# Head outputs of an attention loop: both PSUM halves copied by ScalarE and added by GpSimd

## The chip, the cores and the metric

One Trainium2 chip, one of its cores. The metric is the device time of one execution in microseconds; less is better. The kernel before took 729.84 us, the median of 3 runs (728.89 to 730.41).

## The reference

A decoder layer on a sequence of 1024 tokens and 1024 channels, in float32: an adaptive RMS norm, one projection that feeds a gated convolution and a sparse attention (an indexer picks at most 256 keys for a query), a group norm and gate on each, an output projection, a residual and a last norm. What the change touches is how the attention's values are summed and laid out; what is computed there is:

```
logits = jnp.einsum('bqhd,bqkhd->bqhk', q_b, k_sel).astype(jnp.float32) * att_scale
logits = jnp.where(valid[:, :, None, :], logits, -jnp.inf)
p = jax.nn.softmax(logits, axis=-1).astype(v.dtype)
return jnp.einsum('bqhk,bqkhd->bqhd', p, v_sel)
...
y_attn = group_rmsnorm(y_attn, gn_attn, N_HEADS) * jax.nn.silu(az)
y = jnp.concatenate([y_conv, y_attn], axis=-1) @ w_out
```

There are 8 heads of 64 dimensions. The kernel does not gather keys: it adds a bias of minus a large number to the logits of the keys that were not picked.

## The kernel before

The order of the work is written out by hand: each engine runs its own list of instructions in order, and semaphores alone join the lists. First come the norm and the projection (to about 500 us), then the attention loop (about 505 to 642 us), then the output projection.

Float32 products are made of float32r matmuls on a value's rounded part (names ending in H) and its remainder (ending in L). For the values, VV holds for a head 128 columns: the 64 of the rounded value and the 64 of the remainder. So the sum over keys comes out of TensorE as two groups of 64 PSUM rows, which must be added. In even heads rows 0 to 63 hold the one part and rows 64 to 127 the other, in odd heads the reverse, so that the sum of head h lands on the rows that its output has in ya (rows() in the code). ya[:, t, :] is the pair t of heads 2t and 2t + 1.

A head has 1024 queries in two halves (sb = 0, 1) of 512. A half is numbered g = 2h + sb, 0 to 15; its sum stands in PSUM bank 6 + sb. The loop goes over 96 chunks k, 12 to a head: 4 of the first half and 8 of the second, one for each block of 128 keys. For a chunk:
- TensorE transposes up to four 128x128 blocks of prob into bank 4 + k % 2 (turn, L749);
- ScalarE copies them rounded to phH (split_prob, L1041) and VectorE takes the remainder phL (low_prob, L1382);
- two chunks later TensorE multiplies both with VV (values, L762 and L763).

Two steps x = 2k and x = 2k + 1 belong to a chunk, and tables say at which step of a head the rest is put in the lists. It is for the next head: the logits of its 8 query blocks (logits, L671 and L672), their row maxima on VectorE (row_max, L1374, into nmx) and their exponentials on ScalarE (weights, L982, into prob). An exponential of block i covers (i + 1) x 128 keys, and each is followed by a read of its accumulator. For a block's logits TensorE waits for the exponential two before, which read the same banks. The transposes of a half begin when the exponentials of its four blocks are there.

Four steps after a half's last chunk, ScalarE copies the 64 rows that don't lie where the output does to tmp (other_half, L1050), which has one buffer, and one step later VectorE adds the other 64 rows to it (head_out, L1390), writes ya and raises s_o. For odd g this falls into the third chunk of the next head, ahead of the exponential of its last block (the odd place below); for even g into the third chunk of the second half (the even place). s_o frees tmp for ScalarE, frees the bank for TensorE's sum of the next head, and lets GpSimd square a pair's halves (pair_square, L1601). On the squares TensorE builds the group sums (group_sums, L780), and VectorE's gate multiplies ya in place (pair_gate, L1412) at an even place of heads 2, 4 and 6, where pair_add (L1421) takes the sums out. At the even places of heads 1, 3, 5 and 7 VectorE also copies denominators (keep_den, L1404) instead. At the even places of heads 2 to 5 ScalarE rounds a block of w_out (out_high, L1075), and GpSimd takes its remainder (out_low, L1606).

Of the kernel before, what the change touches and what calls it, by code (L numbers as in the profile page):

```python
# [23 lines left out]
NH = 8  # L24
NIH = 8
NT = 4
# [3 lines left out]
HALF = 512  # L30
# [13 lines left out]
ALU = mybir.AluOpType  # L44
ACT = mybir.ActivationFunctionType
# [102 lines left out]
EXP_AT = (10, 14, 17, 17, 22, 24, 27, 30)  # L148
FIRST_LOGITS = {2: 0, 3: 1, 4: 2, 5: 3, 6: 4, 10: 5, 12: 6, 14: 7}
TMP_AT, OUT_AT = 4, 5  # L150
LAST = 2 * STEPS * (NH - 1)

DSQ_AT = {24 * (2 * t + 1) + (9 if t < NT - 1 else 7): t for t in range(NT)}
# [32 lines left out]
def build(nc, a):  # L186
    with ExitStack() as ctx:
# [96 lines left out]
        tmp = at("tmp", [P, HALF], F32, 76)  # L284
# [5 lines left out]
        ya = at("ya", [P, NT, S], F32, 16)  # L290
# [15 lines left out]
        ps = ctx.enter_context(nc.psum_tensor("ps", [P, 8, HALF], F32))  # L306
# [42 lines left out]
        s_tmp = sem("s_tmp"); s_o = sem("s_o")  # L349
        s_dsq = sem("s_dsq"); s_dt = sem("s_dt"); s_dc = sem("s_dc"); s_dout = sem("s_dout"); s_din = sem("s_din")  # L350
        s_ysq = sem("s_ysq"); s_yss = sem("s_yss"); s_yln = sem("s_yln"); s_yrs = sem("s_yrs")
# [21 lines left out]
        def rows(h):  # L373

            return slice(HD * (h % 2), HD * (h % 2) + HD)
# [15 lines left out]
        OUTS = {2 * last_chunk(g) + 2 + OUT_AT: g for g in range(2 * NH - 1)}  # L391
# [197 lines left out]
        def _(pe):  # L589
# [4 lines left out]
            for j in range(2 * KT):  # L594
                mm = pe.matmul(ps[:, 0, j:j + 1], acc[:, P * j:P * j + P], onesF[:], start=(j == 0), stop=True,
                               skip_group_check=True)
# [6 lines left out]
            for t in range(NB):  # L603
                pe.wait_ge(s_xn, t + 1)
                for kt in range(3):
                    mm = turn_x(kt, t)
                    if t == NB - 1:
                        mm.then_inc(s_xtp, 1)
            for kt in range(3, KT):
                wait_h(pe, kt - 3)  # L610
                for t in range(NB):
                    mm = turn_x(kt, t)
# [81 lines left out]
            for kind, n in SCHEDULE:  # L694
                if kind == "unit":
                    unit(n)
                elif kind == "iwt":

                    pe.wait_ge(s_evac, 1)
                    for b in range(NB):  # L700
                        mm = pe.transpose(ps[:, 4, NIH * b:NIH * b + NIH], Tik[32:40, P * b:P * b + P], identF[32:40, 32:40])
                    mm.then_inc(s_iwt, 1)
                elif kind == "gate":

                    pe.wait_ge(s_gacc, KT)
                    for half in range(2):
                        mm = pe.matmul(ps[0:1, 6 + half, :], onesF[:], gacc[:, HALF * half:HALF * half + HALF], start=True, stop=True)
# [44 lines left out]
            def values(k):  # L752

                h, sb, j, c = CH[k]
                g = 2 * h + sb
                pe.wait_ge(s_pl, k + 1)
                if k == 0:
                    pe.wait_ge(s_vv, NT)
                if j == 0 and g >= 2:
                    pe.wait_ge(s_o, g - 1)  # L760
                out = ps[:, 6 + sb, P * c:HALF]
                pe.matmul(out, VV[:, j, h, :], phH[:, k % NPH, P * c:HALF], start=(j == 0), stop=False, skip_group_check=True)  # L762
                pe.matmul(out, VV[:, j, h, :], phL[:, k % 2, P * c:HALF], start=False, stop=(j == 4 * sb + 3),  # L763
                          skip_group_check=True).then_inc(s_pv, 1)
# [90 lines left out]
        def _(act):  # L855
# [187 lines left out]
            def other_half(g):  # L1043

                h, sb = g // 2, g % 2
                r, d = rows(h), rows(h + 1)
                act.wait_ge(s_pv, last_chunk(g) + 1)
                if g >= 1:
                    act.wait_ge(s_o, g)
                A(tmp[r, :], ps[d, 6 + sb, :], ACT.Copy).then_inc(s_tmp, 1)  # L1050

            def pair_cols(t, half):

# [100 lines left out]
        def _(dve):  # L1154
# [289 lines left out]
            for k in range(len(CH)):  # L1444
                for x in (2 * k, 2 * k + 1):
                    if x % 2:
                        low_prob(k)
                    for u in MAXES.get(x, ()):
                        row_max(u)
                    if x in OUTS:  # L1450
                        head_out(OUTS[x])
                    if x in DSQ_AT:
                        square_den(DSQ_AT[x])
                    if x in KEEP_AT:
                        keep_den(KEEP_AT[x])
                    if x in GATE_AT:
                        pair_gate(GATE_AT[x])
                    if x == LAST + 17:
                        pair_gate(NT - 1, 0)
                    if x in ADD_AT:  # L1460
                        pair_add(*ADD_AT[x])
                    if x in OUT_LOW_AT:
                        low_out(OUT_LOW_AT[x])
                if k == LAST // 2 + 3:
                    low_y(0, 0)
                if k == LAST // 2 + 5:
                    low_y(1, 0)
                if k == LAST // 2 + 11:
                    low_y(2, 0)
# [57 lines left out]
        def _(pool):  # L1527
# [68 lines left out]
            def pair_square(t, half):  # L1596
                pool.wait_ge(s_o, 4 * t + half + 3)
                if t:
                    pool.wait_ge(s_yss, 2 * t + half - 1)
                z = ya[:, t, HALF * half:HALF * half + HALF]  # L1600
                g.tensor_tensor(ysq[half][:], z, z, ALU.mult).then_inc(s_ysq, 1)  # L1601

            def out_low(ct):

                pool.wait_ge(s_woH, ct + 1)
                g.tensor_tensor(hL[:, ct, :], wo[:, ct, :], wo_high(ct).bitcast(F32), ALU.subtract).then_inc(s_woL, 1)  # L1606

            pair_square(0, 0)
            pair_square(0, 1)
            out_low(0)  # L1610
            pair_square(1, 0)
            out_low(1)
            pair_square(1, 1)
            out_low(2)
            pair_square(2, 0)
            out_low(3)
            pair_square(2, 1)
            pair_square(NT - 1, 0)
            pair_square(NT - 1, 1)


INPUTS = ("x", "positions", "w_ada", "w_out", "norm_f", "b_gate", "w_ik", "w_units", "vecs", "ident_f",
# [47 lines left out]
```

## Time and profile before

| what | value |
|---|---|
| median of 3 runs | 729.84 us (728.89 to 730.41) |
| the profiled execution | 727.33 us |
| its span, first to last instruction | 725.5 us |
| granted TensorE clock, mean | 0.991 |
| TensorE busy | 665.0 us (92%) |
| VectorE busy | 490.6 us (68%) |
| ScalarE busy | 365.0 us (50%) |
| GpSimd busy | 228.5 us (31%) |

Shares are over the whole span, in which the stages have different limits. PE is TensorE's matmuls, PEld its weight loads, DVE VectorE, ACT ScalarE, POOL GpSimd. L1050 is line 1050 of the kernel before. A row of the timeline gives start, duration, the instruction, and in brackets the idle time of its engine ahead of it with what ended it. The rows of neighbouring instructions on one engine can overlap a little.

### The profile page before, as it was taken

What the parts mean: (1) busy time and instruction counts of PE and PEld (TensorE: products, weight loads), DVE (VectorE), ACT (ScalarE), POOL (GpSimd) and SP (SyncE); (2) the same over time, 40 slices, a digit from 0 to 9 for tenths busy, and PEclk for the clock granted to TensorE, in tenths of its full rate; (3) what the DMA queues carried; (4) which work ended last, traced back from release to release, by engine and by line L of the source; (5) the groups of instructions that cost most, each with busy time, mean ns of one, the idle gap of its engine ahead of it and who ended that gap; (6) DMA issues with size and microseconds to landing.
All of it is one profiled execution on the core that took longest, in us unless ns stands there. A gap on an engine that the chain in (4) does not pass through costs nothing.

```text
span 725.5 us, 8772 instructions
## 1 busy us (share of the span) xinstructions
PE 665.0 (92%) x3170; PEld 548.3 (76%) x3170; DVE 490.6 (68%) x739; ACT 365.0 (50%) x550; POOL 228.5 (31%) x111
## 2 busy tenths in 40 slices
PE   0379998999999999999999999998998999989996
PEld 0468987878888888888888886886776777778885
DVE  4686814677788999999059753013898989586734
ACT  1484435555664142453543345434878877875212
POOL 0003323532233243658756579530012210000000
PEclk9999999999999999999999999998999999999999
DMA  8902289353323101111110262074853440121431
GB/s 344 414 34 86 57 194 173 116 159 112 96 85 97 63 30 58 44 44 58 32 56 29 87 204 88 30 166 112 293 126 88 117 117 0 60 85 61 174 117 58
DMA packets 22661, 79.14 MB, mean 109 GB/s; under 512 B 3738, under 2 KB 4058, under 8 KB 21596
## 3 DMA queue, kind: packets, MB, share of 16 engines
q1 hardware_dynamic: 22620, 78.60, 35.8%
q8 instruction: 25, 0.41, 0.2%
q14 instruction: 16, 0.13, 0.1%
HBM read 61.77 MB, written 13.41 MB: 104 GB/s over the span
## 4 chain that ended last, share of the span: by engine, by line
PE 71%; DVE 10%; DMA 7%; ACT 5%; issue 4%; SPq 2%; ACTq 0%; DVEq 0%
PE ps L632 15%; PE ps L634 15%; PE ps L633 15%; PE ps L811 4%; PE ps L812 4%; PE ps L813 4%; PE ps L749 4%; DMA iqs<-hlL 3%; PE ps L690 2%; PE ps L691 2%; PE ps L671 2%; PE ps L672 2%; DMA xin<-in_x 2%; DVE phL L1382 2%; DMA wa<-in_w_ada 2%
## 5 line engine op out<-in xcount | busy, mean ns | idle before, releaser
L632 PE MATMUL ps<-hH,wH 128*128 128x512 f32 (+1 forms) x592 | 229.4, 388 | 3.5 <-issue 2.3
L633 PE MATMUL ps<-hL,wH 128*128 128x512 f32 (+1 forms) x592 | 227.4, 384 | 0.0
L634 PE MATMUL ps<-hH,wL 128*128 128x512 f32 (+1 forms) x592 | 227.3, 384 | 0.0
L1532 POOL TENSOR_TENSOR wL<-raw,wH 128x1024 fp32r<-128x1024 f32 x37 | 94.3, 2550 | 185.1 <-ACT wH L866 185.1
L632 PEld LDWEIGHTS ps<-hH,wH 128*128 128x128 f32 x592 | 111.4, 188 | 25.6 <-issue 6.6
L634 PEld LDWEIGHTS ps<-hH,wL 128*128 128x128 f32 x592 | 111.4, 188 | 21.2
L633 PEld LDWEIGHTS ps<-hL,wH 128*128 128x128 f32 x592 | 111.5, 188 | 19.0
L1374 DVE CUSTOM_DVE_ANT_0 ps<-ps,bias 128x128 f32<-128x128 f32 (+3 forms) x64 | 48.7, 761 | 45.6 <-PE ps L672 43.7
L1382 DVE TENSOR_TENSOR phL<-ps,phH 128x512 fp32r<-128x512 f32 (+1 forms) x96 | 52.7, 554 | 21.9 <-ACT phH L1041 17.6
L1021 ACT ACTIVATE relu<-ps,wabs 128x384 f32<-128x384 f32 (+5 forms) x48 | 40.2, 848 | 42.5 <-PE ps L691 19.6
L1268 DVE SCALAR_TENSOR_TENSOR score<-relu,wsgn,score 128x384 f32<-128x384 f32 (+5 forms) x42 | 49.7, 1184 | 16.3 <-ACT relu L1021 13.6
L749 PE MATMUL ps<-identF,prob 128*128 128x128 f32 x288 | 50.7, 287 | 8.5 <-ACT prob L982 4.1
L1289 DVE TENSOR_SCALAR_CACHE_REDUCE above<-score,srch 128x384 bf16<-128x384 f32 (+5 forms) x60 | 56.8, 946 | 2.1
L1041 ACT ACTIVATE phH<-ps 128x512 fp32r<-128x512 f32 (+1 forms) x96 | 46.2, 489 | 20.7 <-PE ps L749 19.4
L982 ACT ACTIVATE prob<-ps,nmx 128x128 f32<-128x128 f32 (+3 forms) x64 | 47.3, 739 | 16.5 <-DVE nmx L1374 16.5
L749 PEld LDWEIGHTS ps<-identF,prob 128*128 128x128 f32 x288 | 35.3, 145 | 24.8 <-DVE phL L1382 13.2
L1601 POOL TENSOR_TENSOR ysq<-ya 128x512 f32<-128x512 f32 x8 | 8.8, 1103 | 138.8 <-DVE ya L1390 138.8
L812 PE MATMUL ps<-hL,yH 128*128 128x512 f32 x128 | 49.9, 390 | 0.0
L866 ACT ACTIVATE wH<-raw 128x1024 fp32r<-128x1024 f32 x37 | 39.0, 1054 | 21.2 <-DMA raw<-in_w_ik 12.1
L762 PE MATMUL ps<-phH,VV 128*128 128x512 f32 (+1 forms) x96 | 39.3, 409 | 0.0
L671 PE MATMUL ps<-ks,qs 128*128 128x512 f32 (+2 forms) x96 | 35.5, 370 | 3.0 <-ACT prob L982 1.8
L763 PE MATMUL ps<-phL,VV 128*128 128x512 f32 (+1 forms) x96 | 33.7, 352 | 0.0
(205 smaller groups left out, 1088.4 us busy)
## 6 DMA issues: line engine op xcount, KB each, us to landing
raw<-in_w_units SPq DMA_DIRECT2D x36, 512.0 KB, 3.4
wa<-in_w_ada SPq DMA_DIRECT2D x8, 1024.0 KB, 8.8
ks<-qk_halves SPq DMA_DIRECT2D x32, 256.0 KB, 5.6
xin<-in_x SPq DMA_DIRECT2D x8, 512.0 KB, 12.6
gw<-in_w_ada SPq DMA_DIRECT2D x8, 512.0 KB, 4.3
qs<-qk_halves SPq DMA_DIRECT2D x16, 256.0 KB, 4.1
wo<-in_w_out SPq DMA_DIRECT2D x8, 512.0 KB, 9.4
xe<-in_x SPq DMA_DIRECT2D x8, 512.0 KB, 4.0
```

Of the source, the lines that this page charges most:

```text
L632: pe.matmul(out, wH[:, n % 2, kt, :], hH[:, kt, cols], start=(kt == 0), stop=False)
L633: pe.matmul(out, wH[:, n % 2, kt, :], hL[:, kt, cols], start=False, stop=False)
L634: mm = pe.matmul(out, wL[:, n % 2, kt, :], hH[:, kt, cols], start=False, stop=(kt == KT - 1))
L671: pe.matmul(dst[:, o:e], q, ks1[h % 2][:, o:e], start=True, stop=False)
L749: mm = pe.transpose(ps[:, 4 + k % 2, P * b:P * b + P], prob_of(sb, b)[:, P * j:P * j + P], identF[:])
L812: pe.matmul(out, yH[b % 4][:, ct, :], hL[:, ct, cols], start=False, stop=False)
L982: A(prob_of(sb, i % 4), logit_bank(u), ACT.Exp, bias=nmx[:, u:u + 1], scale=-1.0, accum_out=den[:, h // 2, h % 2, i:i + 1]).then_inc(s_exp, 1)
L1268: v.scalar_tensor_tensor(score_of(i), relu[:, u % 2, 0:n], wsgn[:, i, h:h + 1], score_of(i), ALU.mult, ALU.add).then_inc(s_score, 1)
L1289: v.tensor_scalar(above[:, 0:(i + 1) * P], score_of(i), cand[:, b:b + 1], None, ALU.is_ge, ALU.add, accum_out=count[:, b:b + 1]).then_inc( ...
L1374: v.tensor_tensor_reduce(src, src, bias_of(i), -ATT_SCALE, 3.0e38, ALU.add, ALU.min, nmx[:, u:u + 1]).then_inc(s_mx, 1)
L1382: v.tensor_tensor(phL[:, k % 2, P * c:HALF], ps[:, 4 + k % 2, P * c:HALF], phH[:, k % NPH, P * c:HALF].bitcast(F32), ALU.subtract).then_in ...
L1532: g.tensor_tensor(wL[:, n % 2, :, :], raw[:, n % NRAW, :, :], wH[:, n % 2, :, :].bitcast(F32), ALU.subtract).then_inc(s_wL, 1)
```

## The change

For g = 0 to 13 (ADDED = 14), ScalarE copies both groups of 64 rows: one to tmp as before, and right behind it the other to its place in ya. It raises s_tmp after the second. GpSimd then adds tmp to ya in place and raises s_o. VectorE's sum is left out for these halves and stays for g = 14 and 15. TensorE waits for s_tmp, and no longer for s_o, before it reuses a half's bank. GpSimd's list is written in another order, since the adds now stand between the squares and the low parts of w_out.

```diff
+ADDED = 2 * NH - 2
...
                 if j == 0 and g >= 2:
-                    pe.wait_ge(s_o, g - 1)
+                    pe.wait_ge(s_tmp, g - 1)
...
-                A(tmp[r, :], ps[d, 6 + sb, :], ACT.Copy).then_inc(s_tmp, 1)
+                mm = A(tmp[r, :], ps[d, 6 + sb, :], ACT.Copy)
+                if g < ADDED:
+                    mm = A(ya[r, h // 2, HALF * sb:HALF * sb + HALF], ps[r, 6 + sb, :], ACT.Copy)
+                mm.then_inc(s_tmp, 1)
...
-                    if x in OUTS:
+                    if x in OUTS and OUTS[x] >= ADDED:
                         head_out(OUTS[x])
...
-            pair_square(0, 0)
-            pair_square(0, 1)
-            out_low(0)
-            pair_square(1, 0)
-            out_low(1)
-            pair_square(1, 1)
-            out_low(2)
-            pair_square(2, 0)
-            out_low(3)
-            pair_square(2, 1)
-            pair_square(NT - 1, 0)
-            pair_square(NT - 1, 1)
+            def head_add(n):
+
+                h, sb = n // 2, n % 2
+                r = rows(h)
+                pool.wait_ge(s_tmp, n + 1)
+                z = ya[r, h // 2, HALF * sb:HALF * sb + HALF]
+                g.tensor_tensor(z, z, tmp[r, :], ALU.add).then_inc(s_o, 1)
+
+            for t in range(NT):
+                if t:
+                    pool.wait_ge(s_ysq, 2 * t)
+                head_add(4 * t)
+                if 1 <= t <= 2:
+                    pool.wait_ge(s_o, 4 * t + 1)
+                    out_low(2 * t - 2)
+                    pool.wait_ge(s_woL, 2 * t - 1)
+                head_add(4 * t + 1)
+                if t < NT - 1:
+                    head_add(4 * t + 2)
+                pair_square(t, 0)
+                if 1 <= t <= 2:
+                    out_low(2 * t - 1)
+                    pool.wait_ge(s_woL, 2 * t)
+                if t < NT - 1:
+                    pool.wait_ge(s_ysq, 2 * t + 1)
+                    head_add(4 * t + 3)
+                pair_square(t, 1)
```

ScalarE's list before, from the odd place (g = 7) to the even place (g = 8); semaphores that an instruction waits for stand in brackets:

```order
L1050 ACTIVATE tmp<-ps 64x512 [waits s_o,s_pv]
L1041 ACTIVATE phH<-ps 128x256 [waits s_pv,s_tp]
L982 ACTIVATE prob_3_123,den<-ps,nmx 128x1024 [waits s_tp,s_mx]
L1041 ACTIVATE phH<-ps 128x128 [waits s_pv,s_tp]
L1041 ACTIVATE phH<-ps 128x512 [waits s_pv,s_tp]
L982 ACTIVATE prob_0_116,den<-ps,nmx 128x128 [waits s_tp,s_mx]
L1041 ACTIVATE phH<-ps 128x512 [waits s_pv,s_tp]
L1050 ACTIVATE tmp<-ps 64x512 [waits s_o,s_pv]
L1041 ACTIVATE phH<-ps 128x512 [waits s_pv,s_tp]
```

The same stretch of ScalarE's list now:

```order
L1051 ACTIVATE tmp<-ps 64x512 [waits s_o,s_pv]
L1053 ACTIVATE ya<-ps 64x512
L1042 ACTIVATE phH<-ps 128x256 [waits s_pv,s_tp]
L983 ACTIVATE prob_3_123,den<-ps,nmx 128x1024 [waits s_tp,s_mx]
L1042 ACTIVATE phH<-ps 128x128 [waits s_pv,s_tp]
L1042 ACTIVATE phH<-ps 128x512 [waits s_pv,s_tp]
L983 ACTIVATE prob_0_116,den<-ps,nmx 128x128 [waits s_tp,s_mx]
L1042 ACTIVATE phH<-ps 128x512 [waits s_pv,s_tp]
L1051 ACTIVATE tmp<-ps 64x512 [waits s_o,s_pv]
L1053 ACTIVATE ya<-ps 64x512
L1042 ACTIVATE phH<-ps 128x512 [waits s_pv,s_tp]
```

The copy to ya stands between tmp and the next phH at both places, with no wait of its own. The 1024-wide exponential is third behind tmp now, where it was second.

GpSimd's list before, from the first square on:

```order
L1601 TENSOR_TENSOR ysq_135<-ya 128x512 [waits s_o]
L1601 TENSOR_TENSOR ysq_136<-ya 128x512 [waits s_o]
L1606 TENSOR_TENSOR hL<-wo,hH 128x1024 [waits s_woH]
L1601 TENSOR_TENSOR ysq_135<-ya 128x512 [waits s_yss,s_o]
L1606 TENSOR_TENSOR hL<-wo,hH 128x1024 [waits s_woH]
```

GpSimd's list now, from the add of g = 3 on:

```order
L1618 TENSOR_TENSOR ya<-ya,tmp 64x512 [waits s_tmp,s_ysq]
L1605 TENSOR_TENSOR ysq_136<-ya 128x512 [waits s_o]
L1618 TENSOR_TENSOR ya<-ya,tmp 64x512 [waits s_tmp,s_ysq]
L1610 TENSOR_TENSOR hL<-wo,hH 128x1024 [waits s_woH,s_o]
L1618 TENSOR_TENSOR ya<-ya,tmp 64x512 [waits s_tmp,s_woL]
L1618 TENSOR_TENSOR ya<-ya,tmp 64x512 [waits s_tmp]
L1605 TENSOR_TENSOR ysq_135<-ya 128x512 [waits s_yss,s_o]
```

Each square now stands right behind the add that completes its half of the pair, and each low part of w_out stands in the longer gap between two adds.

## Rows read from the trace of the kernel before

**Rows 1.** One head: us, then busy us (instructions) of PE, PEld, DVE, ACT, POOL.

```profile
549.55:565.26 15.71, 14.07 (x87) 11.35 (x86) 13.75 (x32) 13.35 (x32) 3.38 (x2) 1.00 0.56 136
```

**Rows 2.** Waits from 510 to 645 us: total us, times, longest.

```profile
DVE phL L1382 <- ACT phH L1041: 13.1, 17, 2.4
...
PE ps L671 <- ACT prob L982: 1.8, 6, 0.3
```

**Rows 3.** Instructions on the tile tmp: min/median/max ns.

```profile
L1050 ACT ACTIVATE tmp<-ps x16: 588/592/596, 508.7 to 641.7; 64x512 f32<-64x512 f32 x16
L1390 DVE TENSOR_TENSOR ya<-ps,tmp x16: 672/684/695, 510.5 to 642.4; 64x512 f32<-64x512 f32 x16
```

**Rows 4.** Timeline, ScalarE, odd place: start us, duration us, instruction, idle before.

```profile
567.95 0.59 ACT L1050 ACTIVATE tmp<-ps 64x512 f32<-64x512 f32 x1
568.56 0.38 ACT L1041 ACTIVATE phH<-ps 128x256 fp32r<-128x256 f32 x1
568.84 1.11 ACT L982 ACTIVATE prob<-ps,nmx 128x1024 f32<-128x1024 f32 x1
569.84 0.20 ACT L982 ACTIVATION_READ_ACCUMULATOR prob<-ps,nmx 128x1 f32 x1
...
570.79 0.60 ACT L1041 ACTIVATE phH<-ps 128x512 fp32r<-128x512 f32 x1 [0.58 <-PE ps L749]
```

**Rows 5.** Timeline, VectorE, odd place.

```profile
568.50 0.14 DVE L1374 DVE_READ_ACCUMULATOR2_ANT nmx<- 128x1 f32 x1
...
571.42 0.69 DVE L1382 TENSOR_TENSOR phL<-ps,phH 128x512 fp32r<-128x512 f32 x1 [0.54 <-ACT phH L1041]
```

**Rows 6.** Timeline, TensorE, odd place.

```profile
570.09 0.66 PE L749 MATMUL ps<-identF,prob 128*128 128x128 f32 x4 [0.30 <-ACT prob L982]
```

**Rows 7.** Timeline, ScalarE, even place of head 3.

```profile
556.54 0.59 ACT L1050 ACTIVATE tmp<-ps 64x512 f32<-64x512 f32 x1
557.29 0.60 ACT L1041 ACTIVATE phH<-ps 128x512 fp32r<-128x512 f32 x1 [0.17 <-PE ps L749]
...
560.93 0.21 ACT L982 ACTIVATION_READ_ACCUMULATOR prob<-ps,nmx 128x1 f32 x1
```

**Rows 8.** Timeline, VectorE, even place of head 3.

```profile
558.64 0.69 DVE L1390 TENSOR_TENSOR ya<-ps,tmp 64x512 f32<-64x512 f32 x1
559.37 0.28 DVE L1404 TENSOR_SCALAR dT<-ps 16x128 f32<-16x128 f32 x1
```

**Rows 9.** Timeline, TensorE, even place of head 3.

```profile
561.21 0.48 PE L671 MATMUL ps<-ks,qs 128*128 128x512 f32 x1
```

**Rows 10.** Timeline, ScalarE, even place of head 1.

```profile
527.45 0.58 ACT L982 ACTIVATE prob<-ps,nmx 128x384 f32<-128x384 f32 x1 [0.29 <-DVE nmx L1374]
```

**Rows 11.** Timeline, ScalarE, even place of head 4.

```profile
573.39 0.60 ACT L1041 ACTIVATE phH<-ps 128x512 fp32r<-128x512 f32 x1 [0.54 <-PE ps L749]
...
577.34 0.20 ACT L982 ACTIVATION_READ_ACCUMULATOR prob<-ps,nmx 128x1 f32 x1
```

**Rows 12.** Timeline, VectorE, even place of head 4.

```profile
573.21 1.28 DVE L1412 SCALAR_TENSOR_TENSOR ya<-ya,vec,azs 128x1024 f32<-128x1024 f32 x1
...
575.00 0.67 DVE L1390 TENSOR_TENSOR ya<-ps,tmp 64x512 f32<-64x512 f32 x1
575.60 0.67 DVE L1421 TENSOR_TENSOR azs<-ps,dden 128x512 f32<-128x512 f32 x1
```

**Rows 13.** Timeline, TensorE, even place of head 4.

```profile
577.41 0.55 PE L749 MATMUL ps<-identF,prob 128*128 128x128 f32 x3
577.71 0.48 PE L671 MATMUL ps<-ks,qs 128*128 128x512 f32 x1
```

**Rows 14.** Timeline, GpSimd, squares and one low part.

```profile
570.32 1.04 POOL L1601 TENSOR_TENSOR ysq<-ya 128x512 f32<-128x512 f32 x1 [7.53 <-DVE ya L1390]
576.25 2.40 POOL L1606 TENSOR_TENSOR hL<-wo,hH 128x1024 fp32r<-128x1024 f32 x1 [4.88 <-ACT hH L1075]
...
643.14 1.54 POOL L1601 TENSOR_TENSOR ysq<-ya 128x512 f32<-128x512 f32 x1 [12.65 <-DVE ya L1390]
```

## The prediction

> **What bounds the kernel now.** I read first the waits and then the timeline, engine by engine, of the attention loop (about 505 to 642 us), since only that stage is touched. In one head's 15.71 us TensorE is busy 14.07, VectorE 13.75, ScalarE 13.35 and GpSimd 3.38 us [rows 1]. Three engines lie within 0.72 us of each other, so the busy shares name no bound, and the waits show a relay: VectorE waits 13.1 us in all for phH, and TensorE waits for exponentials [rows 2]. What counts is which engine hands over last at the points where the change edits a queue. There are two kinds, once a head each.
>
> *The odd place* (end of a head's second half: g = 1, 3, ..., 13). ScalarE runs tmp at 567.95, phH of 256 columns at 568.56, the 1024-wide exponential at 568.84, and its accumulator read ends at 569.84 + 0.20 = 570.04 [rows 4]. TensorE's four transposes start at 570.09, released by that exponential [rows 6]. The row maximum that the exponential also needs was there at 568.50 + 0.14 = 568.64 [rows 5], 0.20 us before it began: ScalarE's queue is late, not VectorE. Behind it VectorE idles 0.54 us until phH comes [rows 5], so time freed on VectorE here ends in that idle.
>
> *The even place* (g = 0, 2, ..., 12). ScalarE has idle time after tmp: 0.17 us in head 3 [rows 7], 0.54 us in head 4 [rows 11]. Here VectorE does the head's sum just ahead of work that TensorE wants, at 558.64 and 575.00 [rows 8, 12].
>
> **What is removed.** 14 of 16 sums on VectorE (684 ns median [rows 3]). From one start to the next such a sum holds VectorE 559.37 - 558.64 = 0.73 us in an odd head and 575.60 - 575.00 = 0.60 us in an even one [rows 8, 12]: about 9.3 us over the loop.
>
> **What is added on ScalarE.** 14 copies of 64x512 right behind tmp. The same shape from the same bank is tmp itself, 592 ns [rows 3], and the next instruction starts 568.56 - 567.95 = 0.61 us after it, while behind phH (0.38 us long) the next starts after 0.28 [rows 4]. So some instructions overlap the one ahead by 0.10 us and tmp does not. The new copy is not in the trace of before: its slot lies between 0.59 - 0.10 = 0.49 and 0.61 us. Unlike tmp it reads and writes the same 64 rows. In even heads these begin at partition 0, as phH's do, and I take 0.49; in odd heads they begin at 64, and I take 0.61, as for tmp. The Trainium skill, "ScalarE: Activation LUTs", in its passage on the ACTIVATE instruction's cost, has back-to-back ACTIVATEs overlap by about 93 ns. The trace agrees behind phH (0.10) and not behind tmp. By the page every copy would take 0.50 us, and the seven odd places would cost 3.5 us.
>
> At the odd place nothing covers the copy: phH, the exponential and TensorE's transposes all move by it. Heads 0, 2, 4, 6 give 4 x 0.49 and heads 1, 3, 5 give 3 x 0.61: **+3.8 us** (bounds 7 x 0.49 = 3.4 and 7 x 0.61 = 4.3). The VectorE slot freed there is worth nothing, for the reason above. If the exponential were late from VectorE instead, the cost would fall by no more than the 0.20 us in hand.
>
> At the even place the copy first fills ScalarE's idle time and VectorE's freed slot counts:
> - g = 2: the 384-wide exponential waits 0.29 us for VectorE [rows 10], so VectorE is late. I use head 3's rows for its first steps: phH comes 0.61 - 0.17 = 0.44 us later and 0.73 us of the sum goes: -0.3.
> - g = 6, 10: the same, but ScalarE then also rounds a block of w_out, and its exponential's read ends at 560.93 + 0.21 = 561.14 [rows 7], just ahead of TensorE's logits at 561.21 [rows 9]. These cannot come earlier than ScalarE: the gain is held there, 0.
> - g = 4, 8, 12: the 0.54 us idle takes the copy. VectorE is ahead by 0.60 us, the transposes (577.41) can move up, but the logits behind them (577.71) [rows 13] need the exponential whose read ends at 577.34 + 0.20 = 577.54 [rows 11]. Left is about 0.15 us each: -0.45.
> - g = 0: ScalarE has no second gap yet; 0.
>
> Bounds for the six: nothing, and the full slots 3 x 0.73 + 3 x 0.60 = 4.0 us.
>
> **GpSimd.** 14 adds of 64x512 with two inputs. The nearest rows are a 128x512 square, 1.04 us, and a two-input pass over 1024 columns, 2.40 us, half of which is 1.20 [rows 14]. I take 1.2. Queued behind the add are the squares; for them wait TensorE's sums and VectorE's gate, here at 573.21 [rows 12]. At the odd place both copies are done by 567.95 + 1.22 = 569.17, the add by 570.4, the square by 571.4, as before (570.32 + 1.04 = 571.36). All of it is covered, with 1.8 us in hand; at 2.4 us an add there would still be 0.6 left. ScalarE's next tmp waits for the add; it starts at 573.39 - 0.54 - 0.59 = 572.26 [rows 11, 3], 1.9 us after the add's end. The low parts of w_out now stand between adds, but only between a head's first and second half, where ScalarE's next tmp is some 12 us away. TensorE's wait for a free bank now ends at the copies instead of the sum; no wait on a sum shows among its waits, so 0.
>
> **Sum.** +3.8 - 0.3 - 0.45 = **+3.0 us**. The profiled execution took 727.33 us (725.5 of span and 1.8 around it); it comes to 730.4. The runs' median is 729.84, 2.5 above the profiled one, and I add the difference to the median: **732.8 us**. Own range of this case: 731.3 (low slot, deeper gains) to 734.6 (every copy 0.61, no gains).
>
> **Rivals.**
> - *The gains at the even places come in full* (no change). For it: TensorE's start may lag the matmuls' modelled rows, so that the limits of 0.1 us I read at 561.21 and 577.54 need not bind. Against: waits of logits on exponentials do show, 6 of them [rows 2]. 3.8 - 4.0 = -0.2: 729.6.
> - *VectorE is the bound and the odd places hide the copy* (faster). For it: after the odd exponential ScalarE idles 0.58 us [rows 4], as much as a copy, and a wait on several semaphores is put to the last by inference. Then only the 4.0 us of the even places count: 725.8. Against: the transposes start 0.05 us behind the read's end, too close for chance.
> - *GpSimd and VectorE block each other* (slower still). The last square beside a VectorE pass took 1.54 instead of 1.04 us [rows 14]. At g = 4, 8, 12 the new add becomes ready within 0.2 us of the gate on VectorE [rows 12]. If the add starts first and the gate must wait, that is 1.04 to 1.2 us three times, in a stretch where VectorE is late: +3.4, 736.2. It decides only where the add is first; by the rows (both copies done at 572.26 + 0.61 + 0.49 = 573.36, the gate at 573.21) the gate is. The Trainium skill, "SBUF — State Buffer", in its part on the engine side, calls the shared port pair an exclusive lock, whoever starts first holding it for the whole instruction, against VectorE passes with two SBUF inputs. By it an add that loses is late by the gate's 1.28 us, which the slack bears.
>
> **Chances.** Forecast 0.60, full gains 0.17, hidden copies 0.15, blocking 0.08. A change within 0.2% (1.5 us) is about what a measurement cannot tell from none. Faster is the third case and some of the second, 0.19; same the rest of the second and the low edge of the first, 0.16; slower 0.65. The range of 728.5 to 735.2 leaves out most of the hidden and the blocking case.
>
> **What the profile after would show.** VectorE's busy time 9.6 us less, ScalarE's 8.3 more, GpSimd's some 16 more. The copy's row at 0.59 us, the next instruction 0.49 or 0.61 behind it. At the odd places the 1024-wide exponential 0.5 to 0.6 us later against its row maximum, and TensorE's transposes with it. The step from odd place to odd place 0.3 to 0.6 us longer. The forecast is wrong if that exponential keeps its distance from the row maximum, if the head's period shrinks, or if the gates or sums wait for GpSimd's squares.

## The result, and the profile after

The changed kernel took 733.38 us, the median of 13 runs (730.23 to 739.08), against 728.02 us for the kernel before, measured beside it (726.11 to 731.16, 13 runs): ratio 1.0082, 95% interval 1.0067 to 1.0097. It is slower by 6.0 us by the ratio and by 5.4 by the medians. The forecast was slower by 3.0 us: the time lies in the forecast range, and the forecast size is half of the measured one. The forecast time of 732.8 us stood on the first three runs' median of 729.84; 3.0 on top of 728.02 would be 731.0.

The profiled execution took 733.8 us, with a span of 731.7 and a mean granted clock of 0.986. Line numbers are those of each kernel: L1051, L1053 and L983 after stand for L1050 (tmp), the new copy and L982 (exponential). First the instructions on ya and tmp (min/median/max ns):

```profile
L1053 ACT ACTIVATE ya<-ps x14: 590/592/595, 510.7 to 623.1; 64x512 f32<-64x512 f32 x14
L1618 POOL TENSOR_TENSOR ya<-ya,tmp x14: 1263/1275/2045, 511.3 to 623.7; 64x512 f32<-64x512 f32 x14
...
L1394 DVE TENSOR_TENSOR ya<-ps,tmp x2: 694/694/695, 634.8 to 648.6; 64x512 f32<-64x512 f32 x2
```

The copy takes 592 ns like tmp [rows 3], GpSimd's add 1275 ns, and two sums are left on VectorE. Next ScalarE's timeline at the odd place of g = 7, to be held against [rows 4]:

```profile
571.07 0.59 ACT L1051 ACTIVATE tmp<-ps 64x512 f32<-64x512 f32 x1
571.68 0.59 ACT L1053 ACTIVATE ya<-ps 64x512 f32<-64x512 f32 x1
572.29 0.38 ACT L1042 ACTIVATE phH<-ps 128x256 fp32r<-128x256 f32 x1
572.57 1.11 ACT L983 ACTIVATE prob<-ps,nmx 128x1024 f32<-128x1024 f32 x1
573.57 0.20 ACT L983 ACTIVATION_READ_ACCUMULATOR prob<-ps,nmx 128x1 f32 x1
...
574.52 0.60 ACT L1042 ACTIVATE phH<-ps 128x512 fp32r<-128x512 f32 x1 [0.58 <-PE ps L750]
```

The next instruction starts 0.61 us behind tmp and 0.61 behind the copy (head 3 is odd). The same stretch at g = 13, in head 6, which is even:

```profile
622.46 0.59 ACT L1051 ACTIVATE tmp<-ps 64x512 f32<-64x512 f32 x1
623.06 0.59 ACT L1053 ACTIVATE ya<-ps 64x512 f32<-64x512 f32 x1
623.55 0.37 ACT L1042 ACTIVATE phH<-ps 128x256 fp32r<-128x256 f32 x1
623.82 1.10 ACT L983 ACTIVATE prob<-ps,nmx 128x1024 f32<-128x1024 f32 x1
```

Here the copy holds ScalarE for 623.55 - 623.06 = 0.49 us. At g = 7 the idle time behind the exponential is 0.58 us as before: everything has moved by the copy, and no gap took it up. VectorE and TensorE at g = 7, against [rows 5, 6]:

```profile
571.65 0.14 DVE L1378 DVE_READ_ACCUMULATOR2_ANT nmx<- 128x1 f32 x1
...
575.15 1.53 DVE L1386 TENSOR_TENSOR phL<-ps,phH 128x512 fp32r<-128x512 f32 x2 [0.89 <-ACT phH L1042]
```

```profile
573.82 0.66 PE L750 MATMUL ps<-identF,prob 128*128 128x128 f32 x4 [0.89 <-ACT prob L983]
```

The row maximum was there at 571.79, 0.78 us before the exponential began; it was 0.20 before the change. TensorE stands idle 0.89 us ahead of its transposes, where it was 0.30; over the seven odd places it is 0.74 to 0.77 us in even heads and 0.89 to 0.91 in odd ones, where it was 0.29 to 0.31. VectorE's idle time has grown from 0.54 to 0.89 us: that is where its freed slot went, with the copy's delay.

The chain of waits says the same. Before, it came over VectorE's row maximum into the odd place (start, us, what):

```profile
568.50 0.14 DVE nmx L1374
568.64 0.42 DVE phL L1382
...
569.84 0.21 ACT prob L982
...
570.09 0.66 PE ps L749 x4
```

Now it stays on ScalarE's list:

```profile
570.83 0.13 ACT prob L983
...
571.07 0.59 ACT tmp L1051
...
571.68 0.49 ACT ya L1053
...
572.29 0.38 ACT phH L1042
572.67 0.31 ACT prob L983
...
573.57 0.21 ACT prob L983
...
573.82 0.66 PE ps L750 x4
```

The even place of head 3 (g = 6), ScalarE and then TensorE, against [rows 7, 9]:

```profile
559.50 0.59 ACT L1051 ACTIVATE tmp<-ps 64x512 f32<-64x512 f32 x1
560.10 0.59 ACT L1053 ACTIVATE ya<-ps 64x512 f32<-64x512 f32 x1
560.72 0.60 ACT L1042 ACTIVATE phH<-ps 128x512 fp32r<-128x512 f32 x1
...
564.02 0.23 ACT L983 ACTIVATION_READ_ACCUMULATOR prob<-ps,nmx 128x1 f32 x1
```

```profile
564.30 0.50 PE L672 MATMUL ps<-ks,qs 128*128 128x512 f32 x1 [0.29 <-ACT prob L983]
```

The idle 0.17 us behind tmp is filled, and the logits now wait visibly for the exponential, whose read ends at 564.02 + 0.23 = 564.25.

The even place of head 4 (g = 8), GpSimd and VectorE:

```profile
577.32 2.04 POOL L1618 TENSOR_TENSOR ya<-ya,tmp 64x512 f32<-64x512 f32 x1 [2.48 <-ACT ya L1053]
```

```profile
576.93 1.28 DVE L1416 SCALAR_TENSOR_TENSOR ya<-ya,vec,azs 128x1024 f32<-128x1024 f32 x1
```

GpSimd's add takes 2.04 us beside the gate instead of 1.28, and the gate keeps its 1.28 us [rows 12]. GpSimd bears the collision. The Trainium skill's rule of the shared port pair ("SBUF — State Buffer", engine side) agrees with this: the one that starts first keeps the pair for its whole instruction. The gate was first, with 0.89 us to go when the add began, and the add took 0.77 us longer.

**Where the time went.** The best ruler in these traces is the start of the 1024-wide exponential, once a head; between two of them lie one even and one odd place. Distances in us, worked out from the timelines:

| from, to | before | after | difference | places |
|---|---|---|---|---|
| span's start to head 0 | 499.46 | 501.07 | +1.61 | none |
| head 0 to 1 | 20.79 | 21.48 | +0.69 | g = 0, 1 |
| 1 to 2 | 15.71 | 16.16 | +0.45 | 2, 3 |
| 2 to 3 | 17.18 | 17.39 | +0.21 | 4, 5 |
| 3 to 4 | 15.70 | 16.47 | +0.77 | 6, 7 |
| 4 to 5 | 17.18 | 17.39 | +0.21 | 8, 9 |
| 5 to 6 | 15.70 | 16.45 | +0.75 | 10, 11 |
| 6 to 7 | 17.19 | 17.41 | +0.22 | 12, 13 |
| head 7 to the span's end | 106.59 | 107.88 | +1.29 | none |

From head 0 to head 7 the loop has lengthened by 3.3 us, where the forecast has 3.0. The other 2.9 us of the two traces lie where no edited instruction stands. Behind the last odd place (g = 13) TensorE's clock is lower. Its two waits there, of which the first was 0.89 us before too and the second 0.29:

```profile
623.62 0.33 PE L750 MATMUL ps<-identF,prob 128*128 128x128 f32 x1 [0.87 <-DVE phL L1386]
...
625.06 0.66 PE L750 MATMUL ps<-identF,prob 128*128 128x128 f32 x4 [0.77 <-ACT prob L983]
```

The windows (columns as in [rows 1], the granted clock ahead of the last two):

```profile
623.00:626.00 3.00, 1.61 (x10) 1.08 (x10) 1.63 (x7) 2.92 (x8) 1.27 (x1) 0.98 0.31 117
626.00:629.00 3.00, 2.61 (x7) 2.03 (x7) 1.08 (x2) 0.87 (x2) 0.00 (x0) 0.50 0.17 63
629.00:632.00 3.00, 3.00 (x19) 2.46 (x19) 1.47 (x3) 2.08 (x3) 0.00 (x0) 0.95 0.00 0
```

From 626 us on, for a little over 3 us, TensorE runs at half of full speed, the lower of its two levels, 1.2 against 2.4 GHz. The trace of before shows 1.00 there throughout. Both traces have the lower level at the loop's start as well, from about 500 and 503 us on, for some 7 us. The 1.61 us before the loop belong to instructions that the change leaves alone; there the window from 130 to 140 us shows 0.66 after, and the one from 120 to 130 us 0.83 before.

### The profile page after: what moved, and what is told of

It reads as the page before. It is cut to its first block, busy times and chain, and to the rows that moved or that the text cites. A ratio compares the mean times of both kernels' runs of the same rounds, so it can differ in the third digit from the quotient of the medians.

```text
span 731.7 us, 8796 instructions
## 1 busy us (share of the span) xinstructions
PE 668.1 (91%) x3170; PEld 550.7 (75%) x3170; DVE 486.0 (66%) x725; ACT 371.2 (51%) x564; POOL 248.9 (34%) x125
## 4 chain that ended last, share of the span: by engine, by line
PE 81%; ACT 8%; DVE 5%; issue 4%; DMA 2%; SPq 0%; ACTq 0%; DVEq 0%
PE ps L633 17%; PE ps L635 17%; PE ps L634 17%; PE ps L812 4%; PE ps L814 4%; PE ps L813 4%; PE ps L750 3%; DMA wa<-in_w_ada 2%; ACT prob L983 2%; PE ps L691 2%; PE ps L692 2%; PE ps L672 2%; PE ps L673 2%; PE ps L763 1%; PE ps L764 1%
## 5 line engine op out<-in xcount | busy, mean ns | idle before, releaser
L1618 POOL TENSOR_TENSOR ya<-ya,tmp 64x512 f32<-64x512 f32 x14 | 20.1, 1437 | 107.9 <-ACT ya L1053 107.9
L983 ACT ACTIVATE prob<-ps,nmx 128x128 f32<-128x128 f32 (+3 forms) x64 | 47.2, 739 | 13.4 <-DVE nmx L1378 12.9
L596 PE MATMUL ps<-onesF,acc 128*128 128x1 f32 x32 | 7.0, 352 | 29.5 <-DVE acc L1180 29.5
```

Of the source, the lines that this page charges most:

```text
L983: A(prob_of(sb, i % 4), logit_bank(u), ACT.Exp, bias=nmx[:, u:u + 1], scale=-1.0, accum_out=den[:, h // 2, h % 2, i:i + 1]).then_inc(s_exp, 1)
```

## The experiments

Three questions: whether ScalarE's place ahead of the exponential is the cost (theory S) or something of VectorE (V) or of load as such (L); whether the lower clock follows from the change (C); and whether a better placing beats both kernels. Each kernel was timed beside the kernel before, in 6 or 12 runs against 17 to 35 of it. Diffs are against the changed kernel; ADDED is the list of halves that ScalarE copies twice and GpSimd adds, and TensorE's bank wait and VectorE's list follow it. With an empty ADDED the kernel does the work of the one before, but GpSimd's list keeps its new order:

```diff
-                    pe.wait_ge(s_tmp, g - 1)
+                    pe.wait_ge(s_tmp if g - 2 in ADDED else s_o, g - 1)
...
-                    if x in OUTS and OUTS[x] >= ADDED:
+                    if x in OUTS and OUTS[x] not in ADDED:
...
             def head_add(n):
+                if n not in ADDED:
+                    return
```

**Even places alone.**

```diff
+ADDED = (0, 2, 4, 6, 8, 10, 12)
```

> ScalarE copies both halves and GpSimd adds only for even g (0 to 12); odd g as before. Theory S (the odd place costs one ScalarE slot, since the 1024-wide exponential stands behind the copy, and the even places give back little): with the odd places as before, the loop should take what the even places gave in the trace of the changed kernel, +0.2 (g = 0), -0.16 (g = 2), three times -0.28 (g = 4, 8, 12) and twice +0.15 (g = 6, 10): -0.5 us, ratio 0.998 to 1.001. Theory V (VectorE's freed time is what counts and the full slots of 0.60 to 0.73 us come in): -4 us, ratio 0.994.

Ratio 1.0005 (0.9991 to 1.0020). The distances from exponential to exponential changed by +0.26, -0.13, -0.07, +0.17, -0.08, +0.17, -0.07: +0.25 us in all, not -0.5. Theory V falls. S's figure was off too: the gains at g = 4, 8, 12 shrink from 0.28 to 0.07 or 0.08 us when VectorE still does the odd sums, so the places do depend on each other.

**Odd places alone.**

```diff
+ADDED = (1, 3, 5, 7, 9, 11, 13)
```

> ScalarE copies both halves and GpSimd adds only for odd g (1 to 13); even g as before. S: 0.49 us in heads 0, 2, 4, 6 and 0.61 in heads 1, 3, 5, +3.8 us in the loop, every distance from one 1024-wide exponential to the next longer by one slot. If in addition the granted clock falls behind the last odd place as in the changed kernel, 1.2 us more: ratio 1.005 to 1.007. V: the freed VectorE slots cancel it, ratio 1.000 or below.

Ratio 1.0068 (1.0047 to 1.0089), median 732.20 us. The distances grew by 0.57, 0.59, 0.46, 0.60, 0.45, 0.59, 0.44: +3.7 us, with the two sizes of the slot in turn. In the trace the clock behind the last odd place is at its lower level again, but over the 6 runs it is 0.991 in the mean, the same as in the 17 runs of the kernel before beside them. So the odd places hold nearly the whole cost, and here most of it without a lower mean clock.

**One copy more at the odd places, nothing taken off VectorE.**

```diff
+ADDED = ()
...
-                if g < ADDED:
+                if g in ADDED or g in (1, 3, 5, 7, 9, 11, 13):
```

> The kernel before with one more ScalarE copy behind tmp at every odd place: it writes the other half to ya, and VectorE then does its sum as before and writes over it. GpSimd adds nothing and VectorE is freed of nothing. S: the same as the odd half of the change alone, +3.8 us in the loop within 0.3, since the freed VectorE slot falls into its own idle time there. V: worse than that kernel by the seven VectorE slots, 4 to 5 us more, ratio 1.011 or above.

Ratio 1.0073 (1.0050 to 1.0097), median 731.59 us; +3.9 us in the loop, 0.2 from the run above. Whether VectorE is freed of seven sums there or not makes little difference while the even places are as before: the slot ends in its idle time. TensorE's row at one of these places reads as it does in the changed kernel:

```profile
571.52 0.66 PE L750 MATMUL ps<-identF,prob 128*128 128x128 f32 x4 [0.90 <-ACT prob L983]
```

**All but the last odd place.**

```diff
+ADDED = tuple(range(13))
```

> The changed kernel, but the half g = 13 (the last odd place) is summed by VectorE as before. S: 0.49 us less than the changed kernel in the loop, +2.8 against before. Theory C (the slower clock behind the last odd place, 1.24 us in the trace of the changed kernel, comes from TensorE's longer idle time there): no clock drop in that stretch, so 1.7 us less in all than the changed kernel, ratio 1.004 to 1.006. If the drop is chance, it shows here or in other kernels as often.

Ratio 1.0057 (1.0040 to 1.0074). No drop behind the last odd place, as expected, but one at another: the transposes that wait 0.90 us at g = 7 then run at the lower level.

```profile
572.95 1.05 PE L750 MATMUL ps<-identF,prob 128*128 128x128 f32 x4 [0.90 <-ACT prob L983]
...
574.23 1.06 PE L750 MATMUL ps<-identF,prob 128*128 128x128 f32 x4
```

```profile
571.00:573.00 2.00, 0.98 (x6) 0.41 (x4) 1.00 (x4) 1.98 (x5) 1.36 (x2) 1.00 0.91 252
573.00:576.00 3.00, 3.00 (x15) 3.00 (x16) 1.03 (x3) 1.66 (x6) 0.95 (x1) 0.51 1.04 235
576.00:578.00 2.00, 2.00 (x10) 1.26 (x10) 2.00 (x4) 1.43 (x3) 0.72 (x1) 0.88 0.77 170
```

Four transposes take 1.05 us instead of 0.66, and that distance is 19.01 us where the changed kernel has 17.39. So the drop is not bound to the last place; the expectation had named a drop elsewhere as the sign of chance. The last distance (g = 12 changed, g = 13 as before) is 16.95 us for 17.19: the gain of 0.24 is there although VectorE does the sum of g = 13. Set against the even places alone, it seems to hang on the sum of the odd place ahead, g = 11; no run tests that by itself.

**The copy behind the exponential.** At the odd places the copy to ya stands at step 7 instead of 4.

```diff
+COPY_AT = 7
...
                 mm = A(tmp[r, :], ps[d, 6 + sb, :], ACT.Copy)
+                if g in ADDED and g % 2:
+                    return
...
+                    if x in COPIES:
+                        late_copy(COPIES[x])
```

> The changed kernel, but at the odd places the copy to ya stands three steps later in ScalarE's list, behind the 1024-wide exponential and the phH of 128 columns; s_tmp is raised there. Theory S (the cost is the copy's place ahead of that exponential): ScalarE idles 0.58 us there, which takes 0.49 in even heads and all but 0.03 in odd ones, so the loop loses the 3.8 us again and keeps the even places' -0.4: 0.0 to -0.6 us against before, no longer TensorE wait, hence no clock drop at an odd place, ratio 0.998 to 1.001. Theory L (ScalarE's load as such counts, wherever the copy stands): +3 us or more, ratio 1.004 or above.

Ratio 0.9998 (0.9981 to 1.0015), median 727.80 us: the whole loss is gone with the same instructions, the same load on each engine and the same 14 adds on GpSimd. Its loop is 0.24 us shorter than before. Theory L falls and S stands. ScalarE at g = 7:

```profile
568.60 0.59 ACT L1053 ACTIVATE tmp<-ps 64x512 f32<-64x512 f32 x1
569.20 0.38 ACT L1044 ACTIVATE phH<-ps 128x256 fp32r<-128x256 f32 x1
569.48 1.11 ACT L985 ACTIVATE prob<-ps,nmx 128x1024 f32<-128x1024 f32 x1
570.48 0.20 ACT L985 ACTIVATION_READ_ACCUMULATOR prob<-ps,nmx 128x1 f32 x1
570.57 0.28 ACT L1044 ACTIVATE phH<-ps 128x128 fp32r<-128x128 f32 x1
570.87 0.59 ACT L1064 ACTIVATE ya<-ps 64x512 f32<-64x512 f32 x1
571.49 0.60 ACT L1044 ACTIVATE phH<-ps 128x512 fp32r<-128x512 f32 x1
```

The exponential is 0.28 us behind phH and 0.88 behind tmp (0.28 and 0.89 in [rows 4]), and the copy fills the 0.58 us that were idle. One place did lose: at g = 13 the late copy stands ahead of ScalarE's copies for the output projection, and TensorE waits 1.56 us where it waited 0.46. From the last exponential to the end this trace takes 107.82 us for 106.59, at full clock behind that wait.

```profile
623.00 0.47 PE L814 MATMUL ps<-hH,yH 128*128 128x512 f32 x1 [1.56 <-ACT yH L1101]
```

**TensorE kept busy while it waits.** The changed kernel with transposes that nothing reads. TensorE's wait for phL (s_pl) moves ahead of them, since they write the bank.

```diff
+                if k >= 2:
+                    pe.wait_ge(s_pl, k - 1)
+                if h and sb and j == 0:
+                    for b in range(6):
+                        pe.transpose(ps[:, 4 + k % 2, P * (b % 4):P * (b % 4) + P], identF[:], identF[:])
                 if j == 0:
                     pe.wait_ge(s_exp, NB * h + 4 * sb + 4 if k else NB)
-                if k >= 2:
-                    pe.wait_ge(s_pl, k - 1)
```

> The changed kernel with six more 128x128 transposes of the identity on TensorE at each odd place, put before its wait for the exponential; they are written to the bank that the next transposes overwrite, and nothing reads them. The wait for the exponential stays. S and theory C (the granted clock falls because TensorE stands idle longer at the odd places): the loop stays at +3.3 us, within 0.3, and no stretch at an odd place shows the lower clock, so the 1.2 to 1.6 us of that drop are gone: ratio 1.004 to 1.006. If the drop has nothing to do with that idle time, it stays, and the ratio is 1.007 to 1.009.

Ratio 1.0038 (1.0024 to 1.0052), median 730.33 us. In its trace every stretch from 510 to 726 us is at 1.00; the distances are those of the changed kernel within 0.04 us but the first (+0.18), and from head 7 to the end it is 106.59 us, as before the change. The mean clock of its 12 runs is 0.993; of the changed kernel's 13 it is 0.987, and of the 35 runs of the kernel before beside it 0.991. The filler is work added, and yet it wins back 0.44% of the 0.82%. It was expected to win less: 1.2 to 1.6 us, against 3.2 by the two ratios. As it also lifts the clock above that of the kernel before, it does more than take back what the longer waits cost.

**tmp behind the exponential as well, in the kernel before.**

```diff
+ADDED = ()
+TMP_ODD, OUT_ODD = 7, 8
```

> The kernel before with tmp three steps and the VectorE sum three steps later at the odd places, both behind the 1024-wide exponential. S: that exponential then waits for its row maximum, which comes only 0.20 us before ScalarE is free, so at most 0.2 us is won at each of seven places: -0.5 to -1.4 us, ratio 0.998 to 0.9995. If ScalarE's queue alone were the limit: a whole slot each, -4 us, ratio 0.994.

Ratio 1.0005 (0.9987 to 1.0022): nothing that can be measured, where 0.998 to 0.9995 was expected. The exponential now waits for its row maximum, as expected:

```profile
566.98 1.12 ACT L984 ACTIVATE prob<-ps,nmx 128x1024 f32<-128x1024 f32 x1 [0.48 <-DVE nmx L1379]
```

Six distances are shorter by 0.06 to 0.12 us each, 0.6 in all; the first one fell by 2.06 us (18.73), and this trace, alone of those so far, kept the full clock at the loop's start. 2.3 us came back behind head 7: tmp delays the output projection's copies (TensorE waits 1.08 us for them), and a stretch of a little over 3 us around 638 us is at the lower level.

**Late copies, and four even places.**

```diff
+ADDED = (1, 3, 5, 7, 9, 11, 13, 2, 4, 8, 12)
+COPY_AT = 7
```

> The late copy at the odd places, and at the even places the change only where the trace of the changed kernel showed a gain: g = 2, 4, 8, 12; g = 0, 6, 10 are summed by VectorE as before. S: 0.2 + 0.15 + 0.15 us less than the late copy at all 14, so -0.5 to -1.1 us against before, ratio 0.998 to 0.9995, the fastest of these. If the places depend on each other, no better than the late copy at all 14.

Ratio 0.9999 (0.9982 to 1.0016), no better than the late copy at all 14, though expected to be the fastest. Its loop is 1.0 us shorter than before, most in the distances with g = 4, 8 and 12 (16.92 for 17.18), but behind head 7 it takes 109.42 us against 106.59, with the lower clock from 621 to 628 us, where TensorE waits for the yH copies that stand behind the late copy:

```profile
622.00 0.76 PE L814 MATMUL ps<-hH,yH 128*128 128x512 f32 x1 [1.56 <-ACT yH L1101]
```

The late copy at all 14 has the same wait of 1.56 us and kept the full clock behind it, so such a wait does not always bring the drop.

**The same with the last odd place as before.**

```diff
-ADDED = (1, 3, 5, 7, 9, 11, 13, 2, 4, 8, 12)
+ADDED = (1, 3, 5, 7, 9, 11, 2, 4, 8, 12)
```

> Late copies at the odd places 1 to 11, g = 13 wholly as before (tmp ahead of the exponential, VectorE's sum), and ScalarE's two copies with GpSimd's add at the even places 2, 4, 8 and 12. The late copy at the last odd place held up ScalarE's yH copies and with them TensorE by about 1.1 us in the trace; that is mended. Theory S: -0.16 - 3 x 0.25 = -0.9 us in the loop and nothing lost behind it, ratio 0.997 to 1.000. If the even places' gains are within noise: 1.000.

Median 726.50 us against 727.42; ratio 0.9980 (0.9967 to 0.9994). It beats both kernels; against the one before the gain is small, 1.5 us by the ratio and 0.9 by the medians. In its trace the six distances from head 1 on are 0.8 us shorter, near the expected 0.9. But g = 2 gives nothing (15.72 for 15.71), and behind head 7 it takes 108.19 us for 106.59, where nothing was to be lost: TensorE is at the lower level from 637 to 641 us. This comes behind a wait that the kernel before has too, at full clock (the second row):

```profile
636.94 0.54 PE L814 MATMUL ps<-hH,yH 128*128 128x512 f32 x1 [1.94 <-DVE azs L1437]
```

```profile
637.84 0.47 PE L811 MATMUL ps<-hH,yH 128*128 128x512 f32 x1 [1.95 <-DVE azs L1421]
```

**Idle transposes in the kernel before, and in that last one.**

```diff
+                if k >= 2:
+                    pe.wait_ge(s_pl, k - 1)
+                if k == 0:
+                    pe.wait_ge(s_exp, NB - 1)
+                if k == 0 or h and sb and j == 0:
+                    for b in range(4 if k else 12):
+                        pe.transpose(ps[:, 4 + k % 2, P * (b % 4):P * (b % 4) + P], identF[:], identF[:])
...
-                if k >= 2:
-                    pe.wait_ge(s_pl, k - 1)
```

> The kernel before with idle transposes of the identity on TensorE: twelve at the start of the loop, after the seventh exponential of head 0, and four at each odd place ahead of the wait. Nothing else changes. Theory C: the lower clock that every trace but one shows at about 500 to 508 us (a loss of about 2 us, by the one trace without it: 18.73 against 20.79 us from the first to the second 1024-wide exponential) goes away or shrinks: ratio 0.996 to 0.999. If the filler only takes TensorE's time and the clock does not follow: 1.000 to 1.002.

Ratio 0.9987 (0.9971 to 1.0003), median 726.28 us: a gain that this measurement does not tell from none. The trace still has the lower clock from about 502 to 506 us, shorter than the 500 to 507 of before, and the first distance is 20.10 us for 20.79. The mean clock of its 12 runs is 0.994, for 0.992 in the 29 of the kernel before.

> Both of these together: theories S and C give -0.9 and -1 to -3 us, ratio 0.994 to 0.998, faster than the kernel before and than the changed one. If neither holds: 1.000.

Ratio 0.9978 (0.9960 to 0.9996), median 726.77 us: faster than the kernel before, not told apart from the version without the filler. Its trace has no lower clock at the loop's start (first distance 18.81), but it lost 2.8 us before the loop, in the projection.

## Why the prediction was right, and what it missed

- **ScalarE is late at the odd place, by 0.20 us against the row maximum.** Right. The late copy takes the cost to nothing, the added copy alone brings it back in full, and with tmp moved too the row maximum ends the wait.
- **The slot: 0.49 in even heads and 0.61 in odd ones, +3.8 us.** Right in both sizes; the odd places alone measured +3.7. All eight copies in even heads of the changed kernel hold ScalarE 0.49 or 0.50 us, the six in odd heads 0.61 or 0.62.
- **VectorE's freed slot is worth nothing there.** Right where the even places are as before: 3.7 against 3.9 us with and without it. With the even places changed too, the gains at g = 4, 8 and 12 are 0.2 us larger each when VectorE is freed of the odd sums as well.
- **The even places give back 0.75 us.** Near in sum and off in the parts. Taking 7 slots of 0.49 or 0.61 from the distances, they gave -0.5, and by themselves, in the run with even places alone, nothing (+0.25): g = 0 cost 0.20 (forecast 0), g = 2 gave 0.16 (0.3), g = 4, 8, 12 gave 0.28 each (0.15), g = 6, 10 cost 0.16 and 0.14 (0). At g = 8 TensorE's logits followed the exponential's read by 0.05 us instead of 0.17, so more was won than I allowed; at g = 6 the limit did bind, and ScalarE's idle time was smaller than the copy, so that the limit itself moved.
- **GpSimd covered, add 1.2 us.** Right: 1.28, and 2.04 beside the gate. No engine waits for an add. In the rival of blocking the order was as the rows said, gate first, and the loss stayed on GpSimd. The case where the add is first was not tried. GpSimd's busy time grew by 20.4 us for the forecast 16: 14 adds of 1.28 and three times 0.77 us beside the gate. VectorE's fell by 4.6 us over the span for the forecast 9.6, because work ahead of the loop that the change leaves alone held it 4.1 us longer in this trace; ScalarE's grew by 6.2 us for 8.3.
- **The rivals.** Full gains at the even places would have been 4.0 us, where 0.5 came. Copies hidden at the odd places would have left TensorE's wait as it was; it grew by 0.59 us at g = 7. Both fell.
- **Sum +3.0, time 732.8.** The loop's +3.3 agrees. That 732.8 lies so near the measured 733.38 is luck in part: two errors of opposite sign met, a base that was 1.8 us too high (729.84 for 728.02) and a difference that was too small. Two small slips have no weight: the slots of VectorE add up to 9.2 us and not 9.3 (eight halves of 0.60, six of 0.73), and the top of the case's own range, every copy 0.61 and no gains, is 729.84 + 4.3 = 734.1 and not 734.6.
- **What the sum lacks.** The measured +5.4 to +6.0 is 2.4 to 3.0 us more than forecast, and one term that I left out is TensorE's clock. The sum priced the longer wait of TensorE at its own length alone. All four kernels with the copy ahead of the exponential show a stretch at the lower level at an odd place, where TensorE stands idle 0.74 to 0.91 us ahead of the transposes for 0.3; the kernel before, the one with even places alone, and the filled one show none there. Over all runs the mean clock is 0.987 for the changed kernel and 0.991 for the 81 runs of the kernel before beside the experiments. In these 81 runs the time falls by some 0.35 us for each 0.001 of mean clock, so that I estimate the clock's part at 1.4 us. The runs at one and the same mean clock of 0.986 differ still: 729.3 us in the median of six before, 733.8 in that of three of the changed kernel. Another 0.25 us lies outside the span (time less span, 2.03 us for 1.78 to 1.80 in the median; 2.0 to 2.1 in the other kernels with 13 or 14 adds). Taken with the loop's 3.3, about 1 us has no cause here.
- **What the filler shows.** It lifts the mean clock from 0.987 to 0.993, which by the same estimate is 2.0 of the 3.2 us between the ratios 1.0082 and 1.0038. That the rest, 2.8 us, comes out at the forecast's own +3.0 is chance in part, since its clock is 0.002 above that of the kernel before, some 0.7 us.

What stays open: each trace is one execution, so how often a drop comes is known only from the mean clocks of the runs, and these are no lower than before (0.991 and 0.990 for 0.991) in two of the four kernels that show one, the odd places alone and all but the last. Drops also come without any change: in the projection, whose instructions are the same in all kernels, two traces show no stretch at the lower level between 2 and 498 us, and five show two. So that a longer wait brings drops is borne out by the changed kernel and its filled version, and how much of the loss it is elsewhere is not shown. The 1.6 us before the loop differ between traces of kernels that are identical there (first exponential at 498.53 to 502.31 us over the eleven further ones), and I count them as scatter. None of the forecast's rivals was a clock.

## What to carry to other kernels

A copy or any short instruction costs what stands behind it in its engine's list. Ahead of the last operand that another engine waits for, 0.5 us is 0.5 us, even if it relieves an engine that is a little busier (VectorE 13.75 against ScalarE's 13.35 us in a head); three steps further down the same instruction was free, because the engine idled there. Where TensorE waits, look at the granted clock of the next microseconds too: a longer wait can cost more than its own length, here an estimated 1.4 of 6.0 us.

## What was not expected of the hardware

- TensorE's granted clock fell to the lower level for a little over 3 us behind a wait that was longer by 0.5 to 0.6 us (0.77 for 0.29 us at g = 13, 0.90 for 0.30 at g = 7), and not at every such place: at one in each of four traces. The drop cost 1.3 to 1.6 us by the distances (107.88 against 106.59, 19.01 against 17.39). It is not tied to that wait alone: behind a wait of 1.94 us that the kernel before has too, one kernel had it and the one before did not.
- Useless transposes in that wait went with a higher clock, 0.993 for 0.987 in the mean of the runs, and with 3.2 us less by the ratios of 1.0082 and 1.0038, for 42 more matmuls.
- How far ScalarE overlaps two instructions seems to depend on their partitions: behind the same 64x512 copy the next starts after 0.49 us if the copy reads and writes from partition 0, as its follower does, and after 0.61 us if it starts at 64. The Trainium skill, "VectorE: DVE Perf Modes", in its section on two Vector instructions with no wait between them, gives such a rule for VectorE, as a model: an instruction whose input or output starts in another quadrant (group of 32 partitions) than the last one used in the same memory starts only when the earlier ones have finished. On ScalarE these rows show the same pattern; no run tested it by itself.
